# Where the split operands stand in on-chip memory: per-stage shifts of `hid` and `hT` in a 12-stage float32 network

## The reference, cut to what matters

```
for i in 0, 1:   x += 0.5 * swiglu(rms_norm(x), w_ffn1)   # FFN, width 2816
                 x += attention or pooling mixer
                 x += 0.5 * swiglu(rms_norm(x), w_ffn2)   # FFN, width 2816
                 x += sigmoid(rms_norm(x) @ gate) * (p @ proj)
then:            nsa mixer, squared-relu MLP (width 4096), fox attention, squared-relu MLP (width 4096)
```

## Time and profile before

| | |
|---|---|
| median of 3 runs | 1662.71 us (1662.34 to 1662.93) |
| the profiled execution | 1661.7 us, its span 1660.0 us |
| TensorE matmul / weight load busy | 1624.5 us (98%) / 1440.9 us (87%), 10390 each |
| VectorE / ScalarE / GpSimd busy | 1030.6 (62%) / 810.1 (49%) / 148.9 us (9%) |
| mean granted TensorE clock | 0.998 |

### The profile page before, as it was taken

How to read it: one execution, slowest core, us unless ns; L and a number is a source line. 1 busy time by engine, 2 the same in 40 slices (tenths; PEclk the granted TensorE clock), 3 DMA queues, 4 the chain that set the end, 5 groups by cost and what they waited for, 6 DMA issues and landing times.

```text
span 1660.0 us, 25696 instructions
## 1 busy us (share of the span) xinstructions
PE 1624.5 (98%) x10390; PEld 1440.9 (87%) x10390; DVE 1030.6 (62%) x1059; ACT 810.1 (49%) x998; POOL 148.9 (9%) x117
## 2 busy tenths in 40 slices
PE   8999999999999999999999999978999999999998
PEld 6888887888889888888888998856999999889997
DVE  6554667754547654568455588766765578666564
ACT  6343567544345533456343556354544466444442
POOL 2000123300002100011000132221000000100000
PEclk9999999999999999999999999999999999999999
DMA  8545452364553554455545444321455545325551
GB/s 304 212 158 202 151 201 77 114 251 174 202 201 129 203 202 177 177 184 215 190 165 202 152 189 153 127 77 54 157 198 196 182 153 203 128 104 201 196 183 52
DMA packets 41212, 282.06 MB, mean 170 GB/s; under 512 B 4592, under 2 KB 4720, under 8 KB 7728
## 3 DMA queue, kind: packets, MB, share of 16 engines
q1 hardware_dynamic: 40752, 279.47, 45.7%
q0 software_dynamic: 384, 1.51, 0.2%
HBM read 279.91 MB, written 1.05 MB: 169 GB/s over the span
## 4 chain that ended last, share of the span: by engine, by line
PE 88%; DVE 5%; ACT 3%; POOL 2%; issue 1%; DMA 0%; SPq 0%; POOLq 0%; DVEq 0%; ACTq 0%
PE ps L393 28%; PE ps L397 27%; PE ps L396 27%; DVE w_lo L1743 1%; PE ps L597 1%; POOL arena L2489 1%; ACT arena L1578 1%; ACT arena L1576 1%; DMA raw<-weights 0%; PE ps L522 0%; PE ps L701 0%; ACT w_hi L1267 0%; ACT arena L1588 0%; DVE stat L2184 0%; PE ps L1054 0%
## 5 line engine op out<-in xcount | busy, mean ns | idle before, releaser
L1743 DVE TENSOR_TENSOR w_lo<-raw,w_hi 128x2048 fp32r<-128x2048 f32 x261 | 594.5, 2298 | 149.9 <-ACT w_hi L1267 149.8
L1267 ACT ACTIVATE w_hi<-raw 128x2048 fp32r<-128x2048 f32 x261 | 491.4, 1908 | 47.5 <-DMA raw<-weights 45.5
L393 PE MATMUL ps<-w_hi,hT 128*128 128x512 f32 (+1 forms) x984 | 384.0, 390 | 9.9 <-DVE hT L1770 7.1
L397 PE MATMUL ps<-w_hi,hT 128*128 128x512 f32 (+1 forms) x984 | 375.0, 381 | 0.0
L396 PE MATMUL ps<-w_lo,hT 128*128 128x512 f32 (+1 forms) x984 | 374.4, 380 | 0.0
L393 PE MATMUL ps<-hT,w_hi 128*128 128x256 f32 x984 | 282.3, 287 | 1.3 <-DVE hT L1770 1.2
L397 PE MATMUL ps<-hT,w_lo 128*128 128x256 f32 x984 | 277.0, 281 | 0.0
L396 PE MATMUL ps<-hT,w_hi 128*128 128x256 f32 x984 | 276.2, 281 | 0.0
L393 PEld LDWEIGHTS ps<-w_hi,hT 128*128 128x128 f32 x984 | 185.9, 189 | 44.4 <-DVE w_lo L1758 7.0
L397 PEld LDWEIGHTS ps<-w_hi,hT 128*128 128x128 f32 x984 | 185.7, 189 | 36.3
L396 PEld LDWEIGHTS ps<-w_lo,hT 128*128 128x128 f32 x984 | 186.2, 189 | 32.0 <-issue 0.7
(11 more groups left out here) (267 smaller groups left out, 1808.8 us busy)
## 6 DMA issues: line engine op xcount, KB each, us to landing
raw<-weights SPq DMA_DIRECT2D x261, 1024.0 KB, 4.8
raw<-weights SPq DMA_DIRECT2D x12, 256.0 KB, 7.1
X<-x SPq DMA_DIRECT2D x4, 256.0 KB, 6.3
out<-X SPq DMA_DIRECT2D x4, 256.0 KB, 2.1
arena<-p POOLq DMA_DIRECT2D x2, 256.0 KB, 5.6
arena<-counts POOLq DMA_DIRECT2D x1, 512.0 KB, 5.0
arena<-nsa_tables POOLq DMA_DIRECT2D x1, 448.0 KB, 6.1
const<-constants SPq DMA_DIRECT2D x1, 300.0 KB, 7.6
```

Of the source, the lines that this page charges most:

```text
L393: mm = nc.tensor.matmul(dst, a_hi, b_hi, start=start, stop=False, skip_group_check=True)
L397: return nc.tensor.matmul(dst, a_lo, b_hi, start=False, stop=stop, skip_group_check=True)
L1267: nc.scalar.activation(unit_cols(w_hi, u, 0, UNIT), raw[:, r * UNIT:(r + 1) * UNIT], ACT.Copy).then_inc(hi_done.sem, 1)
L1743: nc.vector.tensor_tensor(unit_cols(w_lo, u, 0, UNIT), raw[:, r * UNIT:(r + 1) * UNIT], f(unit_cols(w_hi, u, 0, UNIT)), ALU.subtract).then ...
```

## The change

The shifts by stage are other ones, in words of 4 bytes (high half, rest):

| stage | tensor, role | before | after |
|---|---|---|---|
| 0 | `hid` moving / `hT` standing | 16, 16 / none | 8, 8 / 8, 8 |
| 2 | `hid` moving | 0, 4 | 24, 24 |
| 4 | `hid` moving / `hT` standing | 4, 4 / none | 32, 32 / 32, 32 |
| 6 | `hid` moving | 8, 8 | 40, 40 |
| 9 | `hT` moving | 16, 16 | 8, 8 |
| 11 | `hT` moving | 0, 4 | 72, 72 |

`up_rows` now reads `hT_of(s)`. `hid` grows by 24 words and the padding `before_w` of 24 words goes, so that `const` moves on by 96 bytes and `w_hi`, `w_lo` and `hT` stay; `hT` grows by 56 words, so that `raw`, `X`, `arena`, `sil` and `spare` move on by 224 bytes. No instruction is added, removed or reordered.

```diff
-HID_MOVE = {0: (16, 16), 2: (0, 4), 4: (4, 4), 6: (8, 8)}
-H_MOVE = {9: (16, 16), 11: (0, 4)}
+HID_ROOM, H_ROOM = 40, 72
+HID_MOVE = {0: (8, 8), 2: (24, 24), 4: (32, 32), 6: (40, 40)}
+H_MOVE = {0: (8, 8), 4: (32, 32), 9: (8, 8), 11: (72, 72)}
...
-        hid = sb("hid", 2 * HID + P + MOVE, f32r)
+        hid = sb("hid", 2 * HID + P + HID_ROOM, f32r)
         const = sb("const", NCONST)
-        sb("before_w", 24)
         w_hi, w_lo = sb("w_hi", RING * UNIT, f32r), sb("w_lo", RING * UNIT, f32r)
-        hT = sb("hT", 2 * KC * TOKENS + MOVE, f32r)
+        hT = sb("hT", 2 * KC * TOKENS + H_ROOM, f32r)
...
             def ffn(s, u0):
+                h = hT_of(s)
...
-                            mm = three(bank(b0 + tok), lhs(hT_hi, k, tok), lhs(hT_lo, k, tok), unit_cols(w_hi, u, a, 512), unit_cols(w_lo, u, a, 512),
+                            mm = three(bank(b0 + tok), lhs(h[0], k, tok), lhs(h[1], k, tok), unit_cols(w_hi, u, a, 512), unit_cols(w_lo, u, a, 512),
```

## The result

The changed kernel takes 1667.84 us in the median of 7 runs (1666.63 to 1669.47); the kernel before, over its 7 runs, 1662.68 (1660.33 to 1663.09). The ratio is 1.0035, 95% interval 1.0023 to 1.0047: slower by 5.2 us, clear of what can't be told from no change. I had forecast 1659.1 in a range of 1654 to 1664. The profiled execution took 1666.63 us, its span 1664.8.

The account below looks back on a forecast made before the run. TensorE was taken as the bound, its time the sum of matmul pitches. Moving shifts -2.35 and standing shifts -0.9 and -0.3 gave -3.55, or -3.6 us: median 1662.7 to 1659.1, range 1654 to 1664.

Parts of the forecast that it names:

- the standing `hT`: Stages 0 and 4, 512 columns moving: shifting the standing operand gains, -0.9 and -0.3 us, half-priced between full gain and 0.
- the moving shifts: Moving `hid` and `hT` in the FFNs and MLPs: new places change matmul pitches, together -2.35 us.
- The far moving shifts: Stages 2, 6, 11 at 96, 160, 288 bytes: take the 32-byte pitch as odd multiples; -0.56, 0, -0.95 us.
- Rival B: Moving `hid` of stages 2, 4, 6 and `hT` of 11 fall back to aligned pitch: +3.9, 1666.6 us; chance 0.12.
- Stage 0's `hid`: FFN one, `hid` from 64 to 32 bytes, FFN four's arrangement word for word: -0.59 us.
- Stage 4's `hid`: FFN three, `hid` from 16 to 128 bytes, priced between the 64-byte row and aligned: +0.2 us.
- Stage 9: MLP one, `hT` from 64 to 32 bytes: loop -0.75, first 96 matmuls +0.3, sum -0.45 us.
- Rival D: Whole kernel: placement isn't the cause and nothing changes, 1662.7 us; chance 0.09.
- Rival C: The 113.3 ns rhythm of MLP one's start reaches changed moving stages; half of 15 us gained, 1654; chance 0.12.
- The groups that read `const` and `arena`: 304 matmuls in the two largest groups, operands 128 bytes further apart: taken as 0, at most 1.1 us either way.

Follow-up runs that it names:

- experiment 1: The changed kernel with the two standing shifts of `hT` (FFN one and three) undone: 1664.01 us, ratio 1.0011 to the kernel before.
- experiment 2: The kernel before with only the standing shifts of `hT` added (32 bytes in FFN one, 128 in FFN three): 1665.05 us, ratio 1.0021.
- experiment 4: Changed kernel with other shifts: `hid` 256, 224, 64, 192 bytes, standing `hT` 224 and 64, MLPs 32; weights and `hT` 256 bytes further on: 1668.40 us.
- experiment 5: Changed kernel with other shifts: weight ring 32 bytes further on, `hid` moved 0, 32, 64, 96 bytes, the MLPs' `hT` 32 and 96: 1679.80 us.
- experiment 11: The kernel before profiled once more, with no edit: 1664.24 us in one run.
- experiment 6: The changed kernel's layout without shifts by stage, `hid`, weights and `hT` together 32 bytes further on: 1669.59 us in one run.
- experiment 9: Changed kernel with `hT`'s last chunk displaced 128 bytes in FFN one and three; `hid` moved 16 bytes in one and two, 64 in three and four: 1664.72 us.

## Why the prediction was wrong

*The step that failed* is the one on the standing `hT`: "An excess that doesn't grow with the width must come with something that happens once per matmul" and therefore "shifting the standing one by 32 bytes should do what shifting the moving one did". I priced it at -0.9 and -0.3; it measured +2.7 and +2.6 us (experiments 1 and 2 isolate it). That is 6.5 of the 8.7 us between forecast and result; the moving shifts, +0.8 for -2.35, make 3.2, and TensorE's shorter idle time takes some back. The equal excess of 13.3 ns at both widths said only that aligned operands behave alike at both. The runs show that off alignment they part: 256 columns fall to an excess of 10, 512 columns rise to one of 20. The error was also in the bounds. I wrote that the effect lay between the full gain and 0, although an edit that no row shows has to be bounded by a loss too, and no row excluded one. With +1.9 and +1.3, the mirrors of the full gains, as the upper bound in place of 0, the range would have ended 3.2 us higher, at an estimated 1667, within a microsecond of the result, and the chance of slower would not have been 0.10.

*The far moving shifts* were the second miss. "All three are odd multiples of 32 bytes" rested on a single odd multiple. 288 bytes did follow 32 (-0.9 against -0.95), but because distances 256 apart are alike (experiments 4 and 5), not because it is odd. 96 bytes gave 120.1 ns and 160 gave 118.7: +1.2 against -0.56, and +1.1 against 0. Rival B named this mechanism and its places; it was right for 96 and 128 bytes, half right for 160 and wrong for 288. With the gains of the other moving shifts it left the kernel 0.11% slower (experiment 1); the loss of the standing shifts, which B didn't have, came on top.

*What held.* Stage 0's `hid`, taken from an identical arrangement: -0.59 forecast, -0.56 measured. Stage 4's `hid`: +0.2 against +0.5. Stage 9: -0.45 against -0.4, its first 96 going from 11.12 to 11.44 for the forecast 11.42. This last agreement is luck in part: the 11.12 was one launch's, the kernel before took 11.54 in another (experiment 11), and against that the shift gained. Rival D, nothing changes, is refuted. The Trainium skill ("TensorE: Matmul & The Clock Gate", Part 2) states that loading the next tile's weights takes no read bandwidth from the running matmul. The traces don't bear out what the prediction drew from it, a pitch that doesn't depend on placement: moving both operands together changes nothing (experiment 6), and moving one against the other does (experiment 5). What in the chip joins the two reads isn't shown. Rival C's rhythm exists, but no shift tried brought it to all blocks, and for one program it came and went from launch to launch (experiment 11). The groups that read `const` and `arena`, now 128 bytes further apart, kept their pitch: 108.6 ns before and after for the 176 of the earlier trace rows, 111.5 and 111.7 for the 128.

## What to carry to other kernels

Before moving an operand, list each pair of standing and moving operand that it belongs to with the width that moves, and measure one block of each kind: an edit worth 3% of a 256-column pitch cost 3% of a 512-column one. A sweep with one value per identical stage reads six answers out of one profile. Take pitches from looped blocks behind a busy engine, which repeated; of two starts behind a wait, one didn't. When an effect has no row of its own, its bound on the losing side is as large as that on the gaining side.

## What the runs showed of the hardware

In looped blocks at a granted clock of 1.00, by the distance of the moving from the standing operand, modulo 256 bytes:

| distance, bytes | 256 columns, ns | 512 columns, ns |
|---|---|---|
| 0 | 119.8 to 120.0 | 226.7 to 227.3 by block |
| 16 | 118.7 (116.9, or 113.3 and 116.6 in turn, by what ran before) | not tried |
| 32 | 116.7 | 233.3 |
| 48 / 64 / 80 | 118.4 / 117.8 / 119.8 | not tried |
| 96 / 128 | 120.1 / 119.9 (118.7 in two blocks of the changed kernel) | not tried / 232.4 or 233.5 by block |
| 160 / 192 (-64) | 118.7 / 117.8 | not tried / 233.3 |
| 224 (-32) | 118.3 | 233.3 |
| 240 (-16) | not tried | 233.3 and 226.7 in turn |

Outside the loops 64 bytes also gave 113.3 ns (experiment 9). That distances 256 bytes apart are alike was tried at 0, 32 and 64 bytes for 256 columns, and at 0 and 32 for 512. The rows of one profile give the value of one launch, and for some distances of one stage only.

I hadn't expected three things: that the pitch depends on the distance of TensorE's two operands at all, that the sign of the effect turns with the width, and that the same program runs a block at 113.3 or 117.8 ns in two launches. Why 512 columns lose stays open. A weight load is recorded with 0.19 us at either width. That is more than the 0.12 us between two matmuls of 256 columns and less than the 0.23 us between two of 512, a difference that could lie behind it; no run tested that.
